# First sequence's difference-attention value pages: issued by SyncE between the key pages instead of by GpSimd

## What is computed

```python
past = (..., gather_pages(cache_diff_k[l], page_table), gather_pages(cache_diff_v[l], page_table))
k_all = jnp.concatenate([past_k, k_diff], axis=1)
v_all = jnp.concatenate([past_v, v_diff], axis=1)
s = jnp.einsum('bqhcd,bkhcd->bhcqk', q_b, k) * SCALE
p = masked_softmax(s, kp[None, :] <= qp_b[:, None])
p_diff = p[:, :, 0] - lam * p[:, :, 1]
return jnp.einsum('bhqk,bkhe->bqhe', p_diff.astype(v.dtype), v)
```

## Time and profile before

| | us |
|---|---|
| median of 3 executions (1412.35 to 1417.41) | 1412.5 |
| the profiled execution's own time | 1412.28 |
| its span, first to last instruction | 1410.6 |
| TensorE busy | 1375.3 |
| VectorE busy | 467.4 |
| ScalarE busy | 285.5 |
| GpSimd busy | 99.2 |

### The profile page before, as it was taken

How to read it: one execution, slowest core, us unless ns; L and a number is a source line. 1 busy time by engine, 2 the same in 40 slices (tenths; PEclk the granted TensorE clock), 3 DMA queues, 4 the chain that set the end, 5 groups by cost and what they waited for, 6 DMA issues and landing times.

```text
span 1410.6 us, 19613 instructions
## 1 busy us (share of the span) xinstructions
PE 1375.3 (97%) x7357; PEld 602.3 (43%) x7357; DVE 467.4 (33%) x1025; ACT 285.5 (20%) x611; POOL 99.2 (7%) x220
## 2 busy tenths in 40 slices
PE   9999999999999999999999999999999999999987
PEld 4445556777754533333333333333333333333322
DVE  1115484665437432313313213132121231321314
ACT  3005434555541301001101010000101011001002
POOL 2000223434200000000000000000000000000000
PEclk9999999999999999999999999999999999999999
DMA  7336857999998699999999999999999999999995
GB/s 274 119 119 217 277 120 245 328 293 308 359 277 318 282 427 392 423 430 428 428 429 428 428 429 428 428 429 427 429 429 427 429 429 428 429 428 428 429 427 241
DMA packets 75516, 509.39 MB, mean 361 GB/s; under 512 B 19114, under 2 KB 25746, under 8 KB 46130
## 3 DMA queue, kind: packets, MB, share of 16 engines
q1 hardware_dynamic: 60978, 476.30, 83.1%
q0 software_dynamic: 13472, 28.87, 6.4%
q10 hardware_dynamic: 1024, 3.67, 0.7%
HBM read 502.29 MB, written 10.62 MB: 364 GB/s over the span
## 4 chain that ended last, share of the span: by engine, by line
PE 78%; DMA 17%; issue 2%; DVE 2%; ACT 1%; SPq 1%; DVEq 0%; POOL 0%; POOLq 0%; ACTq 0%
PE PS L1510 25%; PE PS L1540 11%; DMA arena<-in_w_gate_up 10%; PE PS L1480 6%; PE PS L367 5%; DMA arena<-in_w_down 5%; PE PS L2232 4%; PE PS L1472 4%; PE PS L630 3%; PE PS L616 3%; PE PS L1367 2%; PE PS L1179 2%; PE PS L382 1%; DMA arena<-in_cache_diff_k 1%; PE PS L1527 1%
## 5 line engine op out<-in xcount | busy, mean ns | idle before, releaser
L1510 PE MATMUL PS<-arena 128*64 128x512 f32 x2048 | 455.8, 595 | 12.2 <-DMA arena<-in_w_gate_up 12.1
L1510 PEld LDWEIGHTS PS<-arena 128*64 128x64 f32 x2048 | 141.5, 137 | 293.6 <-issue 263.8
L1540 PE MATMUL PS<-arena 128*64 128x512 f32 x1024 | 227.1, 594 | 2.7 <-DMA arena<-in_w_down 2.6
L1974 DVE TENSOR_SCALAR arena<-PS 128x512 f32<-128x512 f32 x32 | 22.1, 691 | 444.2 <-PE PS L1519 443.2
L1540 PEld LDWEIGHTS PS<-arena 128*64 128x64 f32 x1024 | 71.6, 137 | 150.7 <-issue 143.5
L1480 PE MATMUL PS<-arena 128*128 128x512 f32 (+1 forms) x180 | 84.2, 608 | 0.0
L1472 PE MATMUL PS<-arena 128*128 128x512 f32 (+1 forms) x192 | 79.4, 617 | 4.5 <-ACT arena L1680 3.7
L367 PE MATMUL PS<-arena 128*128 128x512 f32 (+1 forms) x192 | 77.3, 562 | 1.3 <-DMA arena<-in_w_in 1.3
L1891 DVE TENSOR_TENSOR arena<-PS,arena 128x512 f32<-128x512 f32 (+1 forms) x33 | 22.0, 671 | 167.2 <-PE PS L1488 166.7
L1328 POOL COPY arena<-arena 96x64 bf16 (+1 forms) x34 | 7.9, 234 | 985.8 <-PE PS L1547 941.2
L1665 ACT ACTIVATE arena<-arena 128x512 f32<-128x512 f32 x32 | 20.1, 630 | 266.3 <-DVE arena L1974 266.3
(11 more groups left out here) (299 smaller groups left out, 1271.2 us busy)
## 6 DMA issues: line engine op xcount, KB each, us to landing
arena<-in_w_gate_up SPq DMA_DIRECT2D x128, 2048.0 KB, 20.0
arena<-in_w_down SPq DMA_DIRECT2D x62, 2048.0 KB, 21.8
arena<-in_cache_diff_k SPq DMA_DIRECT2D x64, 256.0 KB, 6.1
arena<-in_cache_diff_v POOLq DMA_DIRECT2D x64, 256.0 KB, 5.1
arena<-in_w_in SPq DMA_DIRECT2D x7, 2048.0 KB, 12.6
arena<-in_cache_cmp_kv POOLq DMA_DIRECT2D x64, 128.0 KB, 3.9
arena<-in_cache_sel_kv SPq DMA_DIRECT2D x64, 128.0 KB, 7.0
arena<-in_w_out SPq DMA_DIRECT2D x1, 4096.0 KB, 14.2
```

Source lines behind the costliest of these rows:

```text
L1510: last = nc.tensor.matmul(bank(2 + role + 2 * u)[64 * h:64 * h + 64], hTm[:, k, BS * u:BS * u + BS], rows[:, D * role + 512 * h:D * role + ...
L1540: last = nc.tensor.matmul(bank(6 + u)[64 * h:64 * h + 64], aT[u][:, c % 4, 64 * (c // 4):64 * (c // 4) + 64], down_w[u][c // 4][:, c % 4, ...
L1974: st(V.tensor_scalar(g1, bank(2 + 2 * u), LIM, None, ALU.min), g1_ready)
```

## The change

The values of a turn's first sequence are issued by SyncE, in `sync_attention`, those of the second still by GpSimd. The helper `value_pages` takes the engine as an argument and is otherwise the old `values_in`, its wait included: the first of the eight waits, outside the prologue, until the last reader of that buffer is done (`l_pv` at `PV_D0` of the turn before for `dv_raw[0]`). In the prologue SyncE takes over the two waits that stood ahead of these pages on GpSimd; GpSimd keeps them too.

```diff
+        def value_pages(eng, pages, i, b, first=False):
+            vd_d = io["cache_diff_v"][0].rearrange("n p h e -> n p (h e)")
+            for pg, page in enumerate(pages):
+                if pg == 0 and not first:
+                    past(eng, l_pv, i * VALUES + ((PV_D1 if b else PV_D0) - VALUES))
+                eng.dma_start(in_runs(dv_raw[b], pg // RUN, pg % RUN), page_runs(vd_d, page)).then_inc(dv_in[2 * b + pg // 4], 16)
...
             dk_pages(0, 1, pages[1], True)
             sp.wait_ge(gate_full, 12)
             win_pages(sp, 0)
+            sp.wait_ge(pv_full, len(STAGES))
+            past(sp, l_tp, NPAGE + group_at("kd0") + 1)
+            value_pages(sp, pages[0], 0, 0, True)
             past(sp, l_sc, SC_DIF)
             with sp.Fori(1, PAIRS_OF_SEQ) as i:
                 pages = [pages_of(SP, i, b) for b in range(2)]
                 dk_pages(i, 0, pages[0])
+                value_pages(sp, pages[0], i, 0)
                 dk_pages(i, 1, pages[1])
                 sel_pages(i, pages)
...
             pool.wait_ge(pv_full, len(STAGES))
             past(pool, l_tp, NPAGE + group_at("kd0") + 1)
-            values_in(pages[0], 0, 0, True)
             for n in (10, 11):
                 gates_stored(pool, n)
             pool.wait_ge(stored, n_stored)
             cmp_pages(pool, pages_of(POOL, 1, 0), 1, 0)
-            values_in(pages[1], 0, 1, True)
+            value_pages(pool, pages[1], 0, 1, True)
...
                 cmp_pages(pool, pages[1], i, 1, range(4))
                 queries_of(i)
                 cmp_pages(pool, pages[1], i, 1, range(4, NPAGE))
-                values_in(pages[0], i, 0)
                 if not last:
                     cmp_pages(pool, pages_of(POOL, i + 1, 0), i + 1, 0)
...
-                values_in(pages[1], i, 1)
+                value_pages(pool, pages[1], i, 1)
```

More of the change, by code:

```diff
@@ L537, in pool_attention @@
         def pool_attention(pool, st):
[L538 to L544, removed]
             def queries_of(i, first=False):
```

## The result

| | before | changed |
|---|---|---|
| median, us, of 4 runs each | 1412.63 (1412.35 to 1417.41) | 1423.76 (1422.38 to 1426.57) |
| ratio, 95% interval | | 1.0072 (1.0052 to 1.0093) |
| the profiled execution's own time | 1412.28 | 1422.38 |
| its span | 1410.6 | 1420.4 |
| TensorE busy | 1375.3 | 1379.9 |

What follows compares the result with a forecast made beforehand. TensorE was taken as the bound, so only its waits for loads in the sample attention could shrink. Keys -1.24, values -0.3, other terms 0 gave -1.5 us: 1410.8 for the profiled execution, 1411.0 us as median, range 1409.5 to 1415.5.

Steps and rivals of the forecast that it cites:

- What bounds the kernel, and the ceiling of the gain: TensorE, busy 1375.3 of 1410.6 us; its waits for loads in the sample attention cap the gain at 1.8 us.
- The buffer is free early; SyncE has idle time; the second keys are not held up: SyncE issues values 3.2 to 4.5 us earlier, in 4.2 us, ready 2.2 us before the second keys; cost 0.
- rival C: SyncE held back by value issues of 1.218 us each, pushing keys by 2.4 us: +6.4 us, 1418.9; chance 0.05.
- Key waits and the second sequence's value wait gone, -1.5: TensorE, sample attention: key waits of 0.35 and 0.89 us gone (-1.24), value wait gone (-0.3).
- rival A: No gain: keys stay late because of compressed pages and the keys themselves, not the values; 1412.5 us, chance 0.20.
- GpSimd's earlier start in turn 1: With one table load fewer, compressed pages start at 300.1 instead of 302.02 us, up to 2.4 us earlier.
- Compressed pages beside values: Two queues crossing in turns 0 to 2: compressed pages delayed 1.5 us (ends 0 and 5.1), costing TensorE nothing.
- The time in hand: Delay of compressed pages that costs TensorE nothing: 3.2 us in turn 0, 3.4 us in turn 1.
- The rule that I weighed instead, on taking turns between queues: DMA engines alternate among queues packet by packet, so compressed pages never wait behind all values; 5.1 us delay not reached.
- the 5.1 us end: Largest delay of compressed pages allowed for, where all the values go first; it would cost 5.3 us.
- Rival B: GpSimd's queue, turns 0 to 2: compressed pages starve beside SyncE's values; 1416.3 us (chance 0.07) or 1427.4 (0.02).
- Its milder half: Compressed pages delayed 5.1 us, all values first: costs 5.3 us against a gain of 1.5, 1416.3 us; chance 0.07.

Runs made afterwards that it cites:

- e1_no_values: The change, with the loads of the first sequence's value pages left out after turn 0; 1411.79 us in one run.
- e8_plain_order: The change, with compressed pages read in plain order (32 rows of 4 KB) instead of as 4 x 8 rows; 1413.98 us, ratio 0.9998.
- e10_before_plain: The kernel before (all values on GpSimd), with compressed pages read in plain order instead of as 4 x 8 rows; 1412.80 us, ratio 0.9998.
- e9_same_queue_plain: As e4_same_queue, with compressed pages read in plain order instead of as 4 x 8 rows; 1414.14 us in one run.
- e4_same_queue: The change, with the second sequence's compressed pages of turns 1 to 3 also issued by SyncE, ahead of the values; 1437.81 us, ratio 1.0166.

## Why the prediction was wrong

**What bounds the kernel, and the ceiling of the gain:** right. The experts' stage did not change, and e1_no_values puts the true ceiling at 0.7 us of the span, under the 1.8 that I allowed.

**The buffer is free early; SyncE has idle time; the second keys are not held up:** right in kind. Values went out at 260.44, 0.7 us past the release at 259.70; that is the shift of the whole timeline against the run before (keys at 226.69 instead of 225.99) and nothing more. Eight issues took 5.98, 5.24 and 5.08 us, not 4.2; the slack of 2.2 us covered it, and rival C did not come.

**Key waits and the second sequence's value wait gone, -1.5:** right for the keys. Those of turn 1 landed in 5.1/5.4/6.2 us against the earlier trace rows, and the waits of 0.35 and 0.89 us are not there, neither here nor in e1_no_values, nor in e8_plain_order, where nothing holds TensorE up. So rival A was wrong as to the cause, though not as to how little it is worth. The wait of 0.31 us for the second sequence's values is gone too, but that is luck: in e8_plain_order, with the same moved pages, it stands in the same place with 0.5 us. These values needed up to 6.6 us to land there and up to 4.8 in the changed kernel; why, no run shows.

**GpSimd's earlier start in turn 1:** half right. VectorE's transposes ended later than I took it, and the start came about 1 us earlier and not 1.9.

**"Compressed pages beside values ... I take a delay of 1.5 us":** this is the step that failed, and the larger part of the miss. The delay measured 5.7 to 7 us (longest landing 9.9 to 11.2 against 4.2 to 4.3), above the 5.1 us that I had called the end of its range. I had summed bytes: 5.1 + 2.6 us of work for all 16 DMA engines, as if every load spread over all of them. That sum fails twice. Even for pages that do spread, the crossing costs 2.6 to 3.9 us (e8_plain_order against e10_before_plain) and not 1.5; by itself this still costs TensorE nothing. The rest, 2 to 4 us more, comes with the 4 x 8 shape, and it is what took the delay past the time in hand.

How the shape does it is shown for SyncE's queue only in part and for GpSimd's not at all. On SyncE's queue four engines fit the numbers: about 90 GB/s, so eight pages (1.05 MB) would be 11.6 us of work for one group of four. On GpSimd's queue, where the change has them, the same pages land in some 3 us when nothing crosses them, so successive pages can't all be waiting for the same four engines; which engines they use no run here shows. And on that queue the 4 x 8 shape also makes more packets (the last section), which e8_plain_order takes away together with it, so the number of engines and the number of packets are not told apart there.

The trace had a hint of it. In the earlier trace rows these pages took 12.3 us to land beside SyncE's pages, in the earlier trace rows 3.5 us; I explained the first away by the length of the queue. In e10_before_plain the pages of the same place land in 5.3/6.8/8.0 us instead of 7.6/12.3/15.7, so a good part of it was the shape.

**The time in hand** was summed too small, which partly hid the error. Delay less TensorE's wait gives 4.1 us in turn 0 (5.7 less 1.6), where I had 3.2, and 4.0 in turn 1, where I had 3.4. In the earlier trace rows two transposes stand as x2 in 1.99 us; the second half of the pages is needed only by the second one, 1.0 us after 268.11.

**The Trainium skill**, "DMA: Bandwidth & Descriptors", section "Why a DMA increments its semaphore by 16 and not by 1", gives the number: the engines of a DMA are the largest k up to 16 that divides the sizes of the slowest dimension of both sides. By that rule 4 and 32 give 4, and 32 and 32 give 16. The runs agree on SyncE's queue: 0.26 of the engines with the first shape, and with the second 24 us less (e9_same_queue_plain). The rule that I weighed instead, on taking turns between queues, was no protection: the delay went past the 5.1 us end all the same, and e4_same_queue, where these two kinds of page have no turns to take, is slower still.

**Rival B's price:** the mechanism, the place, turns 0 to 2 and the order of the waits came as written, with 0.09 of the chance. Its milder half was priced at 5.3 us of TensorE's time against 6.2 measured; part of that is luck, since both the delay (5.1 against 5.7 to 7) and the time in hand were put too small. What it lacked was a second term: behind two of the three waits the clock fell, and the same instructions cost 3.6 us more. With it the rival would have said 1419.9, against the 1422.38 of the profiled execution.

## What to carry to other kernels

Before moving a load into a free stretch, ask of each load that already stands there how it is spread over the DMA engines: a low share may be a narrow load and not an idle fabric. Share and GB/s alone don't tell which. In a window with little else in flight the 4 x 8 pages had 0.26 at 90 GB/s (e4_same_queue, 367 to 372 us) and the plain ones 0.28 at 97 (e10_before_plain, 302 to 305 us). What tells is the rate against the rate of issue: the first left at 90 GB/s while they were issued at 176. Landing times in a stretch that is full say how such a load will bear company. A stall of 1.6 to 2.9 us on a TensorE that is otherwise always busy cost here up to 1.7 us more behind it, or nothing more, so price it with both. And a load that nobody waits for is best left where it harms least, since moving it earlier can only gain what someone waits for.

## What was not expected of the hardware

- Loads of a 4 x 8 row shape, issued at 176 GB/s on SyncE's queue, kept the DMA engines only 0.26 busy (90 GB/s). Kept in order in one queue ahead of the values, VectorE waited 9.3 us for them, against 10.5 us when they crossed the values; e9_same_queue_plain against e4_same_queue is 1414.14 against 1437.81 us from this shape alone.
- The same shape makes more packets on GpSimd's queue. The queue's line in the kernel before and in e10_before_plain, with equal bytes:

```profile
q0 software_dynamic: 13472, 28.87, 6.4%
```

```profile
q0 software_dynamic: 7328, 28.85, 5.9%
```

  That is 6144 packets for 64 compressed pages, 96 a page.
- Whole-width pages suffer from the crossing as well: longest landing 6.2, 6.4 and 5.2 us in turns 0 to 2 (e8_plain_order) against 2.6 us at most without it (e10_before_plain).
- Behind a wait of 1.62 us TensorE's clock was 0.66 in the next window of 3 us (4.31 against 2.81 us for twelve instructions), so the wait cost about twice its length; behind one of 1.67 us a turn later it was 1.00, and the same twelve took 2.81 us. With the first of these waits filled with products that nobody reads, the clock stays at 1.00.
